# Routing of the expert layer: the path from the last norm to the first expert, re-ordered on three engines

## What is computed

```python
def moe_swiglu(hn, router, w1, w3, w2):
    t = hn.reshape(-1, d)
    logits = (t @ router).astype(jnp.float32)
    top_vals, top_idx = lax.top_k(logits, TOP_K)
    top_w = jax.nn.softmax(top_vals, axis=-1)
    gates = jnp.sum(top_w[..., None] * jax.nn.one_hot(top_idx, N_EXPERTS, dtype=jnp.float32), axis=1)
    out = jnp.zeros_like(t)
    for e in range(N_EXPERTS):
        h_e = jax.nn.silu(t @ w1[e]) * (t @ w3[e])
        out = out + gates[:, e:e + 1].astype(t.dtype) * (h_e @ w2[e])
    return out.reshape(bsz, s, d)
```

## Time and profile before

| | |
|---|---|
| median of 3 runs | 2386.1 us (2385.84 to 2388.78) |
| the profiled execution, its own time | 2390.61 us |
| its span in the profile | 2388.8 us |
| mean granted TensorE clock | 0.972 of full speed |
| TensorE busy | 2254.9 us (94%) |
| VectorE busy | 1488.1 us (62%) |
| ScalarE busy | 1164.9 us (49%) |
| last norm's products to first expert product | 1316.6 to 1359.5 us |

### The profile page before, as it was taken

One profiled execution on the slowest core, in us unless ns is written; L12 is line 12 of the kernel. 1 busy time (PEld: TensorE's weight loads), 2 busy tenths in 40 slices (PEclk: granted clock), 3 DMA queues, 4 the chain that ended last, 5 costly groups with the idle time before them and its releaser, 6 DMA issues.

```text
span 2388.8 us, 30264 instructions
## 1 busy us (share of the span) xinstructions
PE 2254.9 (94%) x11540; PEld 1900.9 (80%) x11540; DVE 1488.1 (62%) x1811; ACT 1164.9 (49%) x1392; POOL 20.9 (1%) x13
## 2 busy tenths in 40 slices
PE   7899999899999989899899699999999999999997
PEld 6687777778677878899899588888878787878786
DVE  4443345110245276555554598988888898889886
ACT  1121331221233046443463477777777777777775
POOL 0000000000000011000000000000000000000000
PEclk7899999899999989999999799999999999999999
DMA  9776223354222453355364399999999999989991
GB/s 288 189 248 211 81 96 107 79 146 149 89 88 89 124 156 106 124 193 178 108 197 181 138 345 348 349 365 327 372 323 372 327 363 327 369 324 368 331 359 44
DMA packets 348638, 536.20 MB, mean 224 GB/s; under 512 B 51084, under 2 KB 195392, under 8 KB 348552
## 3 DMA queue, kind: packets, MB, share of 16 engines
q1 hardware_dynamic: 342992, 530.81, 64.8%
q10 hardware_dynamic: 5560, 4.19, 0.6%
HBM read 533.89 MB, written 1.07 MB: 224 GB/s over the span
## 4 chain that ended last, share of the span: by engine, by line
PE 86%; DVE 6%; ACT 3%; issue 2%; DMA 1%; ACTq 0%; SPq 0%; DVEq 0%
PE bank L566 22%; PE bank L605 17%; PE bank L607 16%; PE bank L606 16%; PE bank L725 2%; PE bank L598 1%; ACT w_hi L1739 1%; DVE rstd L1856 1%; PE bank L1155 1%; PE bank L1109 1%; PE bank L574 1%; PE bank L1200 1%; PE bank L689 1%; PE bank L691 1%; DVE w_lo L2417 1%
## 5 line engine op out<-in xcount | busy, mean ns | idle before, releaser
L2417 DVE TENSOR_TENSOR w_lo<-pool,w_hi 128x2048 fp32r<-128x2048 f32 x336 | 765.1, 2292 | 118.5 <-ACT w_hi L1739 118.5
L1739 ACT ACTIVATE w_hi<-pool 128x2048 fp32r<-128x2048 f32 x336 | 643.2, 1917 | 139.4 <-PE bank L607 139.3
L566 PE MATMUL bank<-h,ring 128*128 128x256 f32 (+1 forms) x1968 | 452.4, 387 | 17.9 <-DMA ring<-in_w_in 6.5
L566 PEld LDWEIGHTS bank<-h,ring 128*128 128x128 f32 (+1 forms) x1968 | 373.4, 192 | 89.3 <-issue 26.5
L605 PE MATMUL bank<-w_hi,xe_hi 128*128 128x512 f32 x896 | 357.7, 399 | 8.8 <-DVE w_lo L2417 4.6
L607 PE MATMUL bank<-w_hi,xe_lo 128*128 128x512 f32 x896 | 350.7, 391 | 0.0
L606 PE MATMUL bank<-w_lo,xe_hi 128*128 128x512 f32 x896 | 350.2, 391 | 0.0
L2069 DVE TENSOR_TENSOR piece_lo<-ring,piece_hi 128x1024 fp32r<-128x1024 f32 x118 | 145.1, 1237 | 110.3 <-ACT piece_hi L1302 110.1
L605 PEld LDWEIGHTS bank<-w_hi,xe_hi 128*128 128x128 f32 x896 | 168.9, 188 | 51.6 <-DVE w_lo L2417 11.2
L607 PEld LDWEIGHTS bank<-w_hi,xe_lo 128*128 128x128 f32 x896 | 168.8, 188 | 36.6
L605 PE MATMUL bank<-left_hi,piece_hi 128*128 128x256 f32 x672 | 194.3, 289 | 3.3 <-DVE left_lo L2090 3.3
(11 more groups left out here) (360 smaller groups left out, 2744.6 us busy)
## 6 DMA issues: line engine op xcount, KB each, us to landing
pool<-in_od_exp_w SPq DMA_DIRECT2D x336, 1024.0 KB, 7.0
ring<-in_w_in SPq DMA_DIRECT2D x52, 1024.0 KB, 5.2
ring<-in_ev_ffn_w SPq DMA_DIRECT2D x33, 1024.0 KB, 5.2
ring<-in_w_ada SPq DMA_DIRECT2D x24, 1024.0 KB, 10.0
ring<-in_od_w_in SPq DMA_DIRECT2D x12, 1024.0 KB, 5.3
ring<-in_ev_w_in SPq DMA_DIRECT2D x10, 1024.0 KB, 5.3
ring<-in_w_out SPq DMA_DIRECT2D x8, 1024.0 KB, 5.0
ring<-in_w_in SPq DMA_DIRECT2D x16, 256.0 KB, 4.9
```

Of the source, the lines that this page charges most:

```text
L566: m = nc.tensor.matmul(b[base:base + rows, 0:cols], left(k), right(k), start=(k == 0), stop=(k == K - 1))
L1739: nc.scalar.activation(w_hi[q % 3], ring_slot(q), ACT.Copy)\
L2417: V.tensor_tensor(w_lo[q % 3], ring_slot(q), w_hi[q % 3].bitcast(F32), ALU.subtract).then_inc(item_vector, tick(item_vector, "lo", q))
```

## The change

On TensorE the router becomes the stationary side (8 columns) and `h` the moving one (256 columns). The logits come out as 8 rows; ScalarE copies them to `logit_rows`, and two small transposes bring them back to token rows. The transposes of `x` move behind the position products, and the dummy products move ahead of the gather. The position products, the picks and the gather keep their form.

ScalarE makes the exponential before the eight copies of token rows. It makes no `xe_hi` any more for the first item; VectorE makes both parts. `slot_gate` is cleared by ScalarE.

VectorE clears `item_gate`, `item_pos`, `hid` and `item_expert` before the logits arrive. Finding the best two, choosing, and writing the gates is done for both tiles in one operation where the form allows it. `chosen` is released before the gates are computed. `items` is released as soon as the count is known. The second items are listed afterwards, three at a time, and the gate rows are made after them.

```diff
-        b = claim("gemm", ("logits",), route_ready, "logits")
-        for t in range(NT):
-            for k in range(KD):
-                m = nc.tensor.matmul(b[:, 8 * t:8 * t + 8], h[:, k, P * t:P * t + P], w[:, k], start=(k == 0),
+        b = claim("gemm", ("logits",), route_act, "logits")
+        for k in range(KD):
+            pe.wait_ge(h_ready, when(h_ready, "ffn", 1, k))
+            m = nc.tensor.matmul(b[0:NE, 0:S], w[:, k], h[:, k], start=(k == 0), stop=(k == KD - 1))
...
+        b = claim("gemm", ("logitsT",), route_ready, "logits")
+        pe.wait_ge(route_act, when(route_act, "logits"))
+        for t in range(NT):
+            m = nc.tensor.transpose(b[:, NE * t:NE * t + NE], logit_rows[:, P * t:P * t + P], ident[0:NE, 0:NE])
+        m.then_inc(psum_ready, wrote("logitsT"))
+        token_rows("h", h)
...
         m.then_inc(psum_ready, wrote("pos"))
+        token_rows("x", x)
...
+        pe.wait_ge(consts_set, when(consts_set, "hid"))
+        for n in Y:
+            pe.wait_ge(*busy[n])
+            m = nc.tensor.matmul(bank[n], hid[:, 0:P], hid, start=True, stop=True)
...
         for g, m in gather():
             m.then_inc(psum_ready, wrote("gather", g))
-        pe.wait_ge(consts_set, when(consts_set, "hid"))
-        for n in Y:
-            m = nc.tensor.matmul(bank[n], hid[:, 0:P], hid, start=True, stop=True)
...
+        pe.wait_ge(route_ready, when(route_ready, "items"))
...
+        b = psum(act, "logits")
+        nc.scalar.activation(logit_rows, b[0:NE, 0:S], ACT.Copy).then_inc(route_act, tick(route_act, "logits"))
+        act.wait_ge(route_ready, when(route_ready, "diff"))
+        nc.scalar.activation(route[:, 8:10, 1:2], route[:, 8:10, 0:1], ACT.Exp).then_inc(route_act, tick(route_act, "exp"))
         for name, dst in (("h", h_tok), ("x", acc)):
...
-        act.wait_ge(route_ready, when(route_ready, "diff"))
-        nc.scalar.activation(route[:, 8:10, 1:2], route[:, 8:10, 0:1], ACT.Exp).then_inc(route_act, tick(route_act, "exp"))
-        for g in range(2):
-            psum(act, "gather", g)
-            m = nc.scalar.activation(xe_hi[:, 4 * g:4 * g + 4].rearrange("p a b -> p (a b)"), bank[GB[g]], ACT.Copy)
+        nc.scalar.activation(slot_gate, eps, ACT.Copy, scale=0.0)\
...
+        V.memset(item_gate[:, :, NE:], 0.0)
+        V.memset(item_pos[:, :, NE:], -1.0)
+        V.memset(hid, 0.0).then_inc(consts_set, tick(consts_set, "hid"))
+        V.tensor_copy(item_expert[:, 0:NE].bitcast(I32), iota8)
+        V.memset(item_expert[:, NE:].bitcast(I32), 0).then_inc(route_ready, tick(route_ready, "cleared"))
+        b = psum(dve, "logitsT")
...
+        for t in range(NT):
+            m = V.max(top[:, t], route[:, t, 0:8])
+        link(m)
+        for t in range(NT):
+            m = V.max_index(route[:, 4 + t, 0:8].bitcast(U32), top[:, t], route[:, t, 0:8])
+        V.tensor_tensor(mix[:, :, 0:1], top[:, :, 1:2], top[:, :, 0:1], ALU.subtract)\
+            .then_inc(route_ready, tick(route_ready, "diff"))
+        dve.wait_ge(route_ready, when(route_ready, "diff"))
+        link(V.tensor_copy(ids[:, :, 0:2], route[:, 4:6, 0:2].bitcast(U32)))
+        for t in range(NT):
+            V.tensor_scalar(one[:, t], iota8, ids[:, t, 0:1], None, ALU.is_equal)
+            m = V.tensor_scalar(other[:, t], iota8, ids[:, t, 1:2], None, ALU.is_equal)
+        link(m)
+        V.tensor_tensor(chosen, one, other, ALU.add).then_inc(route_ready, tick(route_ready, "chosen"))
+        dve.wait_ge(route_ready, when(route_ready, "chosen"))
         dve.wait_ge(route_act, when(route_act, "exp"))
+        link(V.tensor_scalar(mix[:, :, 2:3], mix[:, :, 1:2], 1.0, None, ALU.add))
+        link(V.reciprocal(mix[:, :, 3:4], mix[:, :, 2:3]))
+        link(V.tensor_tensor(mix[:, :, 4:5], mix[:, :, 3:4], mix[:, :, 1:2], ALU.mult))
         for t in range(NT):
+            m = V.tensor_scalar(one[:, t], one[:, t], mix[:, t, 3:4], None, ALU.mult)
+        link(m)
+        for t in range(NT):
+            m = V.scalar_tensor_tensor(item_gate[:, t, 0:NE], other[:, t], mix[:, t, 4:5], one[:, t], ALU.mult, ALU.add)
+        link(m)
         b = psum(dve, "pos")
...
+        link(V.scalar_tensor_tensor(item_pos[:, :, 0:NE], b[:, 0:16].rearrange("p (t e) -> p t e", e=8), FAR, chosen,
+                                    ALU.add, ALU.mult))
+        link(V.tensor_scalar(item_pos[:, :, 0:NE], item_pos[:, :, 0:NE], -FAR, None, ALU.add))
...
+        V.tensor_copy(item_count.bitcast(I32), part[:, 0, 0, 0:1]).then_inc(route_ready, tick(route_ready, "items"))
+        dve.wait_ge(route_ready, when(route_ready, "items"))
         link(V.tensor_tensor(rank, rank, second, ALU.subtract))
...
+            m = V.scalar_tensor_tensor(mine[:, j], rank, float(j), second, ALU.is_equal, ALU.mult)
+        link(m)
+        each = [P, MAXI - NE, NE]
+        for t in range(NT):
+            m = V.scalar_tensor_tensor(part[:, :, t], item_pos[:, t, 0:NE].unsqueeze(1).broadcast_to(each), float(-P),
+                                       mine, ALU.add, ALU.mult)
+        link(m)
...
+        for t in range(NT):
+            m = V.tensor_scalar(gate_tok[:, t], iota, item_pos[:, t, 0:1], item_gate[:, t, 0:1], ALU.is_equal, ALU.mult)
+        link(m)
         link(V.tensor_scalar(slots, gate_tok.rearrange("p a b -> p (a b)"), 2.0, None, ALU.is_gt))
...
         for g in range(2):
-            m = V.tensor_tensor(xe_lo[:, 4 * g:4 * g + 4].rearrange("p a b -> p (a b)"), bank[GB[g]],
-                                xe_hi[:, 4 * g:4 * g + 4].rearrange("p a b -> p (a b)").bitcast(F32), ALU.subtract)
+            part_hi, part_lo = (t[:, 4 * g:4 * g + 4].rearrange("p a b -> p (a b)") for t in (xe_hi, xe_lo))
+            psum(dve, "gather", g)
+            link(V.tensor_copy(part_hi, bank[GB[g]]))
+            m = V.tensor_tensor(part_lo, bank[GB[g]], part_hi.bitcast(F32), ALU.subtract)
```

More of the change, by code:

```diff
@@ L300, in two_blocks @@
     slot_gate = few(1)
+    second_id = few(MAXI - NE)
+    logit_rows = rstd[0:NE, 3]
     ssum = few(2)
@@ L2317, in _ @@
         normed(("ffn", 1))
-        b = psum(dve, "logits")
+        V.memset(item_gate[:, :, NE:], 0.0)
[4 more added lines that the diff above has]
+        b = psum(dve, "logitsT")
         V.tensor_copy(route[:, 0:2, 0:8], b[:, 0:16].rearrange("p (t e) -> p t e", e=8))\
@@ L2323, in _ @@
         dve.wait_ge(route_ready, when(route_ready, "logits"))
+        top, ids, mix = route[:, 2:4], route[:, 6:8], route[:, 8:10]
+        one, other, chosen = route[:, 10:12], route[:, 12:14], route[:, 14:16]
         for t in range(NT):
-            link(V.max(route[:, 2 + t, 0:8], route[:, t, 0:8]))
-            link(V.max_index(route[:, 4 + t, 0:8].bitcast(U32), route[:, 2 + t, 0:8], route[:, t, 0:8]))
-            link(V.tensor_copy(route[:, 6 + t, 0:2], route[:, 4 + t, 0:2].bitcast(U32)))
@@ L2360, in _ @@
         m.then_inc(route_ready, tick(route_ready, "picked"))
-        for t in range(NT):
-            link(V.tensor_scalar(gate_tok[:, t], iota, item_pos[:, t, 0:1], item_gate[:, t, 0:1], ALU.is_equal, ALU.mult))
-        second, rank, mine, part = route[:, 0], route[:, 1], route[:, 2], route[:, 3]
+        second, rank, part = route[:, 0], route[:, 1], route[:, 5:11].rearrange("p (j t) e -> p j t e", t=NT)
+        mine, number = route[:, 2:5], route[:, 11:14]
         V.tensor_scalar(second, b[:, 16:24], float(P), None, ALU.is_gt)\
@@ new lines, in _ @@
+        link(m)
[5 more added lines that the diff above has]
+        for t in range(NT):
+            m = V.tensor_reduce(item_pos[:, t, NE:MAXI], part[:, :, t], AX_X, ALU.add)
+        link(m)
+        for t in range(NT):
+            m = V.tensor_tensor(part[:, :, t], item_gate[:, t, 0:NE].unsqueeze(1).broadcast_to(each), mine, ALU.mult)
@@ new lines, in _ @@
+        link(m)
+        for t in range(NT):
+            m = V.tensor_reduce(item_gate[:, t, NE:MAXI], part[:, :, t], AX_X, ALU.add)
+        link(m)
+        link(V.tensor_tensor(number, iota8.unsqueeze(1).broadcast_to(each), mine, ALU.mult))
+        link(V.tensor_reduce(second_id, number, AX_X, ALU.add))
+        link(V.tensor_copy(item_expert[:, NE:MAXI].bitcast(I32), second_id))
+        for t in range(NT):
+            m = V.tensor_scalar(gate_tok[:, t], iota, item_pos[:, t, 0:1], item_gate[:, t, 0:1], ALU.is_equal, ALU.mult)
```

52 lines of the change are left out of this document (6 added, 46 removed).

## The result

| | median | runs |
|---|---|---|
| before | 2387.02 us | 2385.84 to 2388.78 (4) |
| after | 2371.13 us | 2367.14 to 2371.84 (4) |

The ratio is 0.9926, with a 95% interval of 0.9914 to 0.9939: the changed kernel is faster, by 15.9 us between the medians and by 17.7 us by the ratio (0.0074 x 2387). The forecast was 2368.5 in 2364 to 2376. The profiled execution of after took 2367.14 us, with a span of 2365.3; it was the fastest of its four, while that of before (2390.61) was slower than all four runs in the table.

The account below looks back on a forecast made before the run. One chain of small steps, not an engine, was taken to bound the stretch. The terms put the first expert product at 1341.6 against 1359.5, 17.9 us less; from the median 2386.1 this gave 2368.2, called 2368.5, range 2364 to 2376.

Parts of the forecast that it names:

- R to T: From the first router product (R) to VectorE's logits copy (T): T at 1326.3, about 0.6 us gained.
- second part: The stretch T to P, with transposes and position products at full clock: gain about 10.5 us.
- T to P: From VectorE's logits copy (T) to its first operation on the positions (P): 3.6 us, against 14.11 before.
- P to E: From VectorE's first operation on the positions (P) to the first expert product (E): 11.7 us, against 18.46 before.
- cover: VectorE's listing of second items ends before the gather's first half appears, with 0.6 us left.
- Entering the loop: VectorE reads the count and enters its loop ahead of the first lower half: 1.1 us from the copy's end.
- that is their price: Dummy products, moved ahead of the gather, stand in the chain for 1.8 of their 1.98 us.
- Behind E: From the first expert product (E), toward the first scatter product (S): same slow products expected; 2.3 us more if clock holds.
- One: Rival: the clock stays at 1.2 GHz for the whole stretch; gain 8.8 to 12.5, time about 2375.5; chance 0.12.
- Two: Rival: ScalarE's table load starts only behind the difference; 1 us lost, 2369.5; chance 0.05.
- Three: Rival: thin TensorE work before E keeps the clock low far into the first expert; 2389.8; chance 0.03.

Follow-up runs that it names:

- third: The changed kernel again, unchanged, as yardstick of the third series: 2366.48 us, ratio to before 0.9909.
- no_dummy: Changed kernel without the dummy products and the clearing of the result banks; the first gather product gives their count: 2370.84 us, ratio to before 0.9917.
- u_router: Changed kernel with the old router (tokens stationary, 8 router columns moving, no logits copy or small transposes): 2369.68 us, ratio to before 0.9922.
- u_exp: Changed kernel with the exponential back behind all eight token copies on ScalarE: 2374.5 us, ratio to before 0.9937.
- u_xtok: Changed kernel with x's transposes back ahead of the position products: 2370.93 us, ratio to before 0.9917.
- u_dummies: Changed kernel with the two dummy products back behind the gather: 2371.95 us, ratio to before 0.9935.
- u_round: Changed kernel with ScalarE making `xe_hi` again and VectorE only subtracting: 2371.14 us, ratio to before 0.9923.
- again: The changed kernel again, unchanged, as yardstick of the first series: 2368.56 us, ratio to before 0.9922.
- u_items: Changed kernel with the item count released only behind the listing and the slots, as before: 2368.99 us, ratio to before 0.9917.
- combo: Changed kernel with unread products in TensorE's two holes, no dummies, and VectorE reading the count ahead of the rounding: 2365.13 us, ratio to before 0.9897.
- best: Changed kernel with unread products in both holes, no dummies, and the gather waiting only for banks it writes: 2365.61 us, ratio to before 0.9902.
- warm_both: Changed kernel with only unread products added, four ahead of the router and four behind the gather: 2366.11 us, ratio to before 0.9901.

## Why the prediction was right, step by step

**R to T, forecast 6.0, measured 6.59.** The forecast knew that the clock decides, and took a fall some 0.7 us behind R and a return midway. The clock had already fallen 2.5 us before R and came back 4.3 us behind it (0.82 in the microsecond from 1320), so the products and the handover to ScalarE took 5.78 us instead of 5.1; the rest came to 0.81 against 0.9. The gain of this term is 0.05 us, not 0.6. Where the clock did fall behind R (`third`, `no_dummy`), the term is 6.15 and the gain 0.5, so this miss is one of the clock's moment. What the text did not have is that the new router pays behind T: at the place where the old form leaves the clock at 1.2 GHz, the new one hands over at 2.4 (`u_router`, 1.6 us). That sum was inside "at full clock" of the second part, and was not credited to the router.

**T to P, 3.6, measured 3.47.** Its pieces hold within 0.1: chosen out by T + 2.04 (2.1), exponential at T + 0.95 (1.0 to 1.3) with its table loaded ahead, gates until T + 3.42 (3.5), position products at T + 2.10 (2.15) and 1.37 us long (1.4). Of the 10.6 us that this part gave, `u_exp` puts 5.5 on the place of the exponential. The other 5.1 are the pairing of the tiles, the early release of `chosen`, x's transposes and the clock; x's transposes are worth 1.47 of it (`u_xtok`) and the clock 1.53 (`u_router`). The pairing was not undone by itself. Before, the position products too ran at 1.2 GHz, in a low stretch from 1338.0 to 1348.2 that took in the gather: first product to P took 2.38 us, against 1.37 in after.

**P to E, 11.7, measured 11.51.** Dummies to P + 3.61 (3.7), listing to P + 4.94 (5.1), cover 0.55 (0.6), second half visible at P + 7.21 (7.5). Entering the loop was undersized: the second rounding ends at 1333.97 and the first lower half starts at 1335.23, 1.26 us where 1.1 was taken. The errors partly cancel. (The terms of the text add up to 11.6; it has 11.7.)

One step was wrong in sign. The text let the dummies stand in the chain, "and that is their price". Their place is a gain of 1.3 us, because behind the gather they would hold ScalarE's first upper half, and because without them ahead of it the gather waits for the copies of x anyway (`u_dummies`, `no_dummy`). That second wait is missing from the text: it counted three copies of x, for the dummies' banks, but the gather waits for all banks and so for the fourth copy, which ends at P + 2.5. The forecast of E was not hurt, since it was summed for the new order only.

**Behind E**, 5.8 us at half clock were expected, and about 3.2 were seen (1337.58 to 1340.8), which gave 1.2 us more than forecast: E to S is 12.52 instead of 13.71, and 11.30 where no product is slow. The 1.19 us are half of the 2.5 us by which the slow stretch is shorter. How long it lasts is no constant: the clock falls between 2.5 us ahead of E (`u_round`) and 0.4 us behind it (`no_dummy`), 0.2 ahead in after and 1.1 in before, and comes back between 3.2 us (after, `again`, `u_items`) and 6.1 us (`u_xtok`) behind it. TensorE's idle stretch ahead of E is 4.3 us in after, `again`, `u_router` and `u_dummies` alike, yet the clock is back 3.2, 3.2, 4.7 and 5.4 us behind E. E to S goes with the return: 12.52 and 13.88 at the two ends. What sets the moment of the fall and of the return stays open. It nearly repeats for one kernel (12.52 in after and `again`, 12.61 in `third`), but there is only one profile of before. So the 1.2 us are luck as far as the forecast goes.

**The rivals.** One is out: the clock is 1.00 from 1321 to 1337, sixteen microseconds with nothing on TensorE but transposes, 8-column products, four dummy passes and the gather. The rule of the Trainium skill that stood beside it (page "TensorE: Matmul & The Clock Gate", section "Part 4: PE-mode transpose": transposes do not count as busy work) is not borne out: in before the clock came back at 1331.1, with nothing but transposes on TensorE for the 4.4 us ahead of it. Two is out: the table load at 1322.18 stands ahead of the difference (1323.37 on VectorE). Three is out: the clock was low for less of the first item than before, 3.2 us behind E instead of 5.8.

**What is shown and what is argued.** Single undos sum to 1.6 + 4.9 + 1.3 + 0.1 + 0.6 + 2.4 = 10.9 of the 17.6 us from R to E. The other 6.7 are put down to the shortened VectorE chains, the clearing moved to an idle stretch, and what two undos share; these were argued from the rows and not taken apart. The largest is the listing: its `slots` were written at P + 11.0 before (1351.78 and 0.30) and at P + 4.9 after, 6.1 us earlier. No run undoes that, nor the pairing of the tiles.

**The number.** The parts add up to 21.3 us from R to E and 21.57 were measured, so the sum was right, with errors that cancel by some tenths only: R to T was 0.6 too short, the other two terms together 0.3 too long. The time as such shows less: the median of the same kernel lies at 2371.13, 2368.56 and 2366.48 in three series, so how near it came to 2368.5 is in part luck.

## What to carry to other kernels

Where no engine is full, cut the stretch at the hand-overs and sum each piece from instruction spacings: that gave 21.3 us for one of 21.6, with the clock's moments as the part that no row foretold. When something is moved off the front of a waiting chain, ask what bounds it next before calling it a price or a gain; here a wait of 1.25 us for banks that another engine frees came up when the dummies were taken away (`u_dummies`, `no_dummy`, `combo`), until the gather waited for its own banks only (`best`). And where TensorE must idle for some microseconds, unread products in the hole can be worth more than shortening the work beside it: from R to S `warm_both` is 3.3 us shorter than after and 3.0 shorter than `third`, by the marks; the times don't show it.

## What the runs showed of the hardware

- The granted clock fell to 1.2 GHz around both idle holes of TensorE (3.75 and 4.3 us), but at different moments of the same hole: 2.5 us before R in after, in the first microsecond behind R in before, `third`, `no_dummy` and `u_router`. It also fell 5.4 us into the hole of 6.10 us in before, and 1.3 us behind the hole of 3.06 us in `u_exp`. With products in the holes (`combo`, `warm_both`, `best`) it stayed at 2.4 GHz.
- It stayed at 1.2 GHz through the last 6.0 of 6.6 us of uninterrupted 8-column products and all 16 transposes behind them (`u_router`), and came back 4.0 to 4.4 us behind R in all nine profiles with the 256-column products and a low clock, wherever it had fallen.
- A float32 copy with rounding, PSUM to SBUF, 128x512, takes VectorE 0.69 us, like the difference of that shape (ScalarE: 0.60).
- Between the last rounding and the first lower half VectorE takes 1.26 us, 1.15 of them from the start of the last difference, with the reading of the count and the entry into the loop in between. With the reading moved ahead of the rounding (`combo`) the 1.15 became 0.61, and 0.97 us of idle time appeared where it then stood.
- A table load moved ahead of its operation's wait by itself, right behind the operation ahead: 1322.18 against a release at 1323.5. In `u_router`, where no copy of the logits stands between, it began at 1317.85, right behind the square root.
